# A two-block transformer step: activation stages at 512 columns, a third value stage in two half passes, and a new tail

## The reference

```
s1, s2 = q.k1, q.k2            # 8 heads, 128 keys each; top 16 of each, top 16 of the 256 sums
experts = e1 * 128 + e2        # 16,384 experts; gates = softmax(scores), 128 per token
a = einsum('td,tkd->tk', h, w_u[experts])
y = einsum('tk,tkd->td', gates * gelu(a), w_v[experts])
out = rmsnorm(x + y) * g_final
```

## Time and profile before

| | |
|---|---|
| Time, median of 3 runs | 3456.82 us (3452.38 to 3457.64) |
| Profiled execution: its own time, its span | 3448.67 us, 3446.9 us |
| PE busy, share of the span | 3105.9 us, 90% |
| DVE busy | 2007.6 us, 58% |
| ACT busy | 1343.6 us, 39% |
| POOL busy | 57.2 us, 2% |
| DMA, mean of the span | 155 GB/s |
| Mean granted TensorE clock | 0.954 of full |

### The profile page before, as it was taken

The page is one execution under the profiler, slowest core; times in us unless marked ns, Lnnn a source line. Parts: engine busy times, 40 slices in busy tenths (PEclk is TensorE's granted clock), DMA queues, the critical chain, the costliest instruction groups (busy, mean ns, idle before and its releaser), DMA issues. The chain is left out here.

```text
span 3446.9 us, 50034 instructions
## 1 busy us (share of the span) xinstructions
PE 3105.9 (90%) x20098; PEld 2737.8 (79%) x20098; DVE 2007.6 (58%) x2533; ACT 1343.6 (39%) x1461; POOL 57.2 (2%) x44
## 2 busy tenths in 40 slices
PE   6797895889987989898799889999999999999598
PEld 5675784678876778776699889988998889988486
DVE  3446456544566544444457967744775467744844
ACT  3434343444334443434434434434333433334044
POOL 0000000000000000000000000000000000000501
PEclk9898997999999999999899999999999999999699
DMA  5352453144443354344244444455444554455154
GB/s 215 127 185 86 146 198 120 54 167 168 161 150 110 122 183 177 135 171 147 100 163 167 158 147 158 169 183 193 163 166 166 191 181 164 164 181 191 55 193 136
DMA packets 80592, 535.34 MB, mean 155 GB/s; under 512 B 9960, under 2 KB 13664, under 8 KB 20064
## 3 DMA queue, kind: packets, MB, share of 16 engines
q1 hardware_dynamic: 72576, 520.98, 42.6%
q10 hardware_dynamic: 7904, 12.83, 1.1%
HBM read 530.57 MB, written 3.15 MB: 155 GB/s over the span
## 5 line engine op out<-in xcount | busy, mean ns | idle before, releaser
L1686 DVE TENSOR_TENSOR w_lo<-raw,w_hi 128x2048 fp32r<-128x2048 f32 (+2 forms) x500 | 1130.5, 2262 | 1210.8 <-ACT w_hi L1158 1208.5
L1158 ACT ACTIVATE w_hi<-raw 128x2048 fp32r<-128x2048 f32 (+2 forms) x500 | 945.2, 1891 | 1643.3 <-PE ps L642 660.0
L640 PE MATMUL ps<-w_hi,hT_hi 128*128 128x512 f32 (+3 forms) x1728 | 679.1, 393 | 84.7 <-DVEq L588 72.7
L641 PE MATMUL ps<-w_lo,hT_hi 128*128 128x512 f32 (+3 forms) x1728 | 669.4, 387 | 0.0
L642 PE MATMUL ps<-w_hi,hT_lo 128*128 128x512 f32 (+3 forms) x1728 | 668.6, 387 | 0.0
L1034 PE MATMUL ps<-hT_hi,w_hi 128*128 128x256 f32 x2048 | 590.3, 288 | 13.8 <-DVE w_lo L1686 10.6
L1035 PE MATMUL ps<-hT_lo,w_hi 128*128 128x256 f32 x2048 | 580.5, 283 | 0.0
L1036 PE MATMUL ps<-hT_hi,w_lo 128*128 128x256 f32 x2048 | 579.8, 283 | 0.0
L640 PEld LDWEIGHTS ps<-w_hi,hT_hi 128*128 128x128 f32 x1728 | 330.3, 191 | 157.1 <-DVEq L588 51.8
L1034 PEld LDWEIGHTS ps<-hT_hi,w_hi 128*128 128x128 f32 x2048 | 393.2, 192 | 19.7 <-issue 17.8
L1061 PE MATMUL ps<-w_hi,c_hi 128*128 128x512 f32 x1024 | 400.4, 391 | 6.9 <-DVE c_lo L2438 6.9
(11 more groups left out here) (246 smaller groups left out, 2574.8 us busy)
## 6 DMA issues: line engine op xcount, KB each, us to landing
raw<-in_w_u_t SPq DMA_DIRECT2D x128, 1024.0 KB, 4.7
raw<-in_w_v SPq DMA_DIRECT2D x128, 1024.0 KB, 5.2
raw<-in_w_in_2.0 SPq DMA_DIRECT2D x32, 1024.0 KB, 4.7
raw<-in_odd_w.0 SPq DMA_DIRECT2D x20, 1024.0 KB, 4.7
raw<-in_even_w.0 SPq DMA_DIRECT2D x20, 864.0 KB, 4.4
raw<-in_even_w.3608 SPq DMA_DIRECT2D x16, 1024.0 KB, 4.8
raw<-in_w_out.0 SPq DMA_DIRECT2D x16, 1024.0 KB, 4.8
raw<-in_w_out.1 SPq DMA_DIRECT2D x16, 1024.0 KB, 4.7
```

Of the source, the lines that this page charges most:

```text
L640: pe.matmul(o, hi, wh, start=(c == 0), stop=False)
L641: pe.matmul(o, hi, wl, start=False, stop=False)
L1158: act.activation(w_hi[:, s % 2, 0:size], raw[:, s, 0:size], ACT.Copy).then_inc(hi_done, 1)
L1686: dve.tensor_tensor(w_lo[:, s % 2, 0:size], raw[:, s, 0:size], w_hi[:, s % 2, 0:size].bitcast(F32), ALU.subtract).then_inc(lo_done, 1)
```

## The change

- **Activation stages 1 to 3** use one tile `hT` with `hi` and `lo` side by side: `w_hi` meets both in one matmul of 512 columns, `w_lo` meets `hT_hi` in one of 256, so an item has 32 matmuls in place of 48. The two halves of the bank are added by DVE (`add_halves`, a reduction over pairs, 512 values in and 256 out), and Gelu then works from SBUF in place. Stage 0 stays as it was.
- **The third value stage** (`HALVED` = 2) goes over its 32 rows twice, each pass with half of the columns of `w_v`; an item now holds two rows of 1024 columns, and there are again 32 items of 1 MB. A pass needs four banks, so two are free for the last part's gates, which are built between the two rows of each item. The stage of its own for the last gates is gone, and with it POOL's part in it. Only two banks are flushed, at the start of the second pass.
- **Tail:** POOL multiplies 1024 of the 2048 columns by `g_final`, DVE does the others together with the scaling in one operation; the square root's table is loaded ahead; the first statistics are made among the additions; SP issues two of the four stores. `g_final` is loaded at the start of the fourth value stage.

The core of the diff (PE, DVE and ACT of the value stage, and the activation stages; ACT's and SP's loops over passes are like PE's):

```diff
-    hT_hi = sb("hT_hi", [P, KC, S], F32R)
-    hT_lo = sb("hT_lo", [P, KC, S], F32R)
+    hT = sb("hT", [P, KC, 2, S], F32R)
+    hT_hi, hT_lo = hT[:, :, 0], hT[:, :, 1]
...
+            if (what, q) == ("V", HALVED):
...
+                            rows = src[bass.ds(8 * i + (q * QTR + 2 * s), 2)][:, :, 1024 * (1 - k):1024 * (2 - k)]
+                            sp.dma_start(raw[:, s].rearrange("p (a c) -> p a c", a=2), rows.rearrange("a p c -> p a c")
+                                         ).then_inc(landed[s], 16)
...
         def activations(i, s, q):
...
+            if q > 0:
+                pe.wait_ge(sums_done, 4 * i + ((q - 1) * QTR + s + 1))
+                for k in range(KC):
+                    pe.matmul(ps[:, s % 2, :], wh, hT[:, k].rearrange("p n t -> p (n t)"), start=(k == 0), stop=False,
+                              skip_group_check=True)
+                    mm = pe.matmul(ps[:, s % 2, 0:S], wl, hT_hi[:, k], start=False, stop=(k == KC - 1),
+                                   skip_group_check=True)
+                mm.then_inc(item_used, 1)
+                return
...
+        def half_outputs(i, s, k, first=False):
+            pe.wait_ge(lo_done, 4 * i + (v_first[HALVED] + 16 * k + s + 1))
+            for j in range(2):
+                if j == 1:
+                    if first and k == 1:
+                        pe.wait_ge(flushed, 4 * HALVED + 2)
+                    dense(i + 4 * k, s, PARTS - 1, 2 * k)
+                pe.wait_ge(c_lo_done, 8 * i + (c_first[HALVED] + 32 * k + 2 * s + j + 1))
+                for t in (1, 0):
...
+                    for m in range(2):
...
+                        pe.matmul(o, ch, wh, start=first and j == 0 and t == 0, stop=False, skip_group_check=True)
+                        pe.matmul(o, ch, wl, start=False, stop=False, skip_group_check=True)
+                        mm = pe.matmul(o, cl, wh, start=False, stop=False, skip_group_check=True)
+                mm.then_inc(item_used if j else c_used, 1)
...
+        def half_step(i, s, k, end=False):
+            half_high(i, s, k, 1)
+            split(i + (v_first[HALVED] // 4 + 4 * k + (s + 1) // 4), (s + 1) % 4, 2048)
+            if not (end and s == 3):
+                half_high(i + (s + 1) // 4, (s + 1) % 4, k, 0)
...
+        def add_halves(i, s, q):
+            dve.wait_ge(item_used, 4 * i + (u_first[q] + s + 1))
+            dve.tensor_reduce(CTS[q % 2][:, bass.ds(4 * i + s, 1)].rearrange("p a t -> p (a t)"),
+                              ps[:, s % 2, :].rearrange("p (n t) -> p t n", n=2), AX, ALU.add).then_inc(sums_done, 1)
...
+        def half_step(i, s, k, end=False):
+            half_low(i, s, k, 1)
+            if k == 1 and isinstance(i, int) and i + s == 0:
+                for b in (2, 3):
...
+                    dve.tensor_tensor(xs, xs, ps[:, b, :], ALU.add).then_inc(flushed, 1)
+            if not (closing and k == 1):
+                hots(i + 4 * k + (s + 1) // 4, (s + 1) % 4, g)
...
+            split(i + (v_first[HALVED] // 4 + 4 * k + (s + 1) // 4), (s + 1) % 4, 2048)
+            if not closing:
+                half_low(i + (s + 1) // 4, (s + 1) % 4, k, 0)
...
+            if not (closing and k == 1):
+                weigh(i + 4 * k, s, g, 2 * k)
...
+        for b in range(5):
+            bank_ends(b).then_inc(fin_add, 1)
+        variance(0)
+        bank_ends(5).then_inc(fin_add, 1)
+        inverse(0)
+        for b in range(6, 8):
+            bank_ends(b).then_inc(fin_add, 1)
...
+        scaled(0)
+        variance(1)
+        inverse(1)
+        scaled(1)
```

More of the change, by code:

```diff
@@ L179, in build_in @@
     bank_done = sem("bank_done")
+    c_used = sem("c_used")
     fin_add = sem("fin_add")
     fin_mul = sem("fin_mul")
+    fin_r = sem("fin_r")
     x_in = sem("x_in")
@@ L557, in _ @@
                                  ).then_inc(landed[s], 16)
+        for t in range(NT):
+            sp.wait_ge(dve_out, t + 1)
+            sp.dma_start(out[0, t * P:(t + 1) * P, 1024:2048], x[:, t, 1024:2048]).then_inc(out_done, 16)
     AT_MEM_ROOTS, AT_MEM_HEADS, AT_MEM_TURN, AT_MEM = 2, 3, 5, 7
@@ L1084, in _ @@
         for q in range(PARTS):
+            if q == HALVED:
+                for k in range(2):
+                    for s in range(RAW):
+                        half_outputs(0, s, k, s == 0)
+                    with pe.Fori(1, HLOOPS) as i:
+                        for s in range(RAW):
+                            half_outputs(i, s, k)
+                continue
             for s in range(RAW):
@@ L1611, in _, with half_high @@
         st.meet()
+        def half_high(i, s, k, j):
+            if j == 0:
+                act.wait_ge(c_used, 4 * i + (16 * k + s))
+            elif not isinstance(i, int) or 16 * k + 4 * i + s > 0:
+                act.wait_ge(item_used, 4 * i + (v_first[HALVED] + 16 * k + s))
+            act.activation(c_hi[:, j], CTS[HALVED % 2][:, bass.ds(8 * i + (2 * s + j), 1)].rearrange("p a t -> p (a t)"),
+                           ACT.Copy).then_inc(c_hi_done, 1)
+        def half_step(i, s, k, end=False):
[3 more added lines that the diff above has]
+                half_high(i + (s + 1) // 4, (s + 1) % 4, k, 0)
+            elif k == 0:
+                half_high(0, 0, 1, 0)
         for q in range(PARTS):
@@ L1656, in _ @@
     def _(pool):
[L1658 to L1665, removed]
-        pool.wait_ge(fin_in, 16)
[L1668 to L1672, removed]
+        pool.wait_ge(fin_in, 16)
+        for t in range(NT):
+            for b in range(4 * t, 4 * t + 2):
+                pool.wait_ge(fin_add, b + 1)
+                piece = slice((b % 4) * 512, (b % 4 + 1) * 512)
+                pool.tensor_tensor(XG[:, t, piece], x[:, t, piece], GFIN[:, piece], ALU.mult).then_inc(fin_mul, 1)
     @block.vector
@@ L2407, in step @@
                 if more:
-                    hots(i + (s + 1) // RAW, (s + 1) % RAW, g, q is None)
-                if q is not None and more:
+                    hots(i + (s + 1) // RAW, (s + 1) % RAW, g)
                     u_split(i, s, q)
+                elif g == HALVED:
+                    hots(0, 0, g + 1)
+                add_halves(i, s, q)
                 weigh(i, s, g)
[L2413 to L2417, removed]
+            hots(0, 0, g)
             with dve.Fori(0, LOOPS - 1) as i:
```

152 lines of the change are left out of this document (102 added, 50 removed).

## The result

The changed kernel takes 3400.4 us, median of 4 runs (3398.19 to 3401.74), beside 3454.95 of the kernel before: a ratio of 0.9845, 95% interval 0.9832 to 0.9857, so 54.5 us faster. The forecast was 3390, a gain of 67, with 3376 to 3412 as its range.

A forecast was written before the change was run, and what follows sets the result against it. PE was taken to bound the activation and value stages. Gains of 20.5, 43.0 and 3.5 us sum to 67, giving 3382 for the profiled execution and 3390 as the median, with 3376 to 3412 as the range.

The forecast's parts named there:

- rival A: Half passes: DVE's order sets the pace, costing 5 to 16 us, most likely 3400 us in all; chance 0.13.
- Part 2, the last gates in the half passes: Third value stage: gate stage's 65.5 us removed, gate groups add 23.4; net gain 43.0 us, V3's start included.
- the flush: Start of the third value stage's second pass: DVE flushes two banks and is late for the next item by 1.2 us.
- The chain: Half passes: the dependent steps of an item take 6.12 us where PE wants them at 6.17; it just fits.
- The loads in pieces of 4 KB: Third value stage: 1 MB loads land in between 5.2 and 6.0 us, hidden; zero cost.
- Part 1, the activation stages: Activation stages 1 to 3: an item's matmuls take 5.55 us for 5.76; gain 20.5 us over 96 items.
- Rival C: Activation stages: 512 columns cost nearly what two times 256 do, so a gain of 4 us, 3407 us; chance 0.04.
- Part 1, the chain: Activation stages: with table loads in each loop body, sums come at 12.9 us, needed at 13.3; no loss.
- rival B: Activation stages: a reduction of 1.2 us makes PE wait, costing 38 us over 24 bodies, 3428 us; chance 0.07.
- Part 3, the tail: From last matmul to last store: 6.2 us instead of 9.65, a gain of 3.5 us, between 1 and 6.
- V3's slow start: First 15 matmuls of the last value stage: 5.97 us would become 3.40, a gain of 2.6 us.
- Rival D: Half passes: the low clock comes in with the gates, 154 us more, 3544 us, slower than before; chance 0.03.

The follow-up runs named there:

- the kernel with all three edits: Changed kernel plus grouped widths, w_lo ahead of the one-hot operations, and a later third operation of the first gate group; the last run: 3390.76 us (0.9818).
- the grouped kernel: Changed kernel with each activation item's 16 matmuls of 512 columns first and its 16 of 256 columns behind them: 3393.75 us (0.9835).
- two and two: Changed kernel with activation matmuls in turns of two of 512 columns, then two of 256: 3397.8 us (0.9839).

## Why the prediction was nearly right

The sum was made for the profiled execution and gave 3382; that took 3398.19, 16 us more: 11.9 in part 1, 3.8 in part 2, 0.8 in the stages ahead. The median came within 10 of 3390 because it lay only 2 us above its profiled execution, where the forecast had added 8. That much is luck. And 3400 is where the prediction had put rival A, while what was found of A is 3.15 us.

**Part 2, the last gates in the half passes: right, and short by 3.8 us of 40.4.** The 65.5 us went, an item costs 5.44 plus 0.75 at best (6.19, predicted 6.17), the flush 1.25 (an item of 7.50 in the second run, against 6.25; predicted 1.2). The stage was to take 197.4 + 1.2 + 0.5 = 199.1 us and took 204.7. Of the 5.6 between, 3.15 is DVE's order, as the runs show (2.3 of it late `c_lo`, 0.9 the flush). The other 2.5 is a slow start at the low clock: in the kernel with all three edits, which has neither, V2 takes 199.11, the sum of the prediction. The kernel before had a slow start of 1.7 in the same place (3191.43 - 3015.65 = 175.8 for 174.1), so the gain fell short by 3.8 only. The chain was computed at 6.12 for a need of 6.17 and the margin was not there in every second item. Rival A was right in kind, and far smaller than its 5 to 16 us. The loads in pieces of 4 KB landed in 5.5 us against 5.2 of whole rows, inside the bounds, and nothing waited for them:

```profile
raw<-in_w_v SPq DMA_DIRECT2D x29, 1024.0 KB, 5.5
```

**Part 1, the activation stages: right in sign, the step that failed is the item's price.** "16 x (0.2267 + 0.12) = 5.55 us" took the step of each width from a stage in which that width stands alone. Alternating, the pair costs 0.354 us and an item 0.10 more; that is 9.6 us over 96 items, and the grouped kernel gave it back (0.347, 6.25). Another 1.2 us is U3's late end, below. The last 1.1 is in small things: even the grouped item gains 0.20 over the kernel before and not 0.213, and U1 and U2 end 0.15 us later each behind their last gate group (2.54 for 2.39). Rival C, which had part 1 bring 4 us and got a chance of 0.04, was nearer to the 8.6 than the forecast's 20.5, and what it says of the steps came true in kind: 0.236 for 512 columns in these stages, against 2 x 0.12. It did not name the cause, the alternation; 512 columns do cost 0.227 where they stand in a row. By the formula for an isolated matmul of the Trainium skill's page "TensorE: Matmul & The Clock Gate", section "Back-to-back issue gap", they would cost 0.216; the trace does not agree.

**Part 1, the chain.** It held, as forecast: PE waited nowhere for the reduction at 0.68 us. The 0.4 us that it was to have to spare were not measured by themselves. But it was walked as if every loop body reloaded ACT's tables; only U1's do, also in the kernel before. So rival B's 38 us at 1.2 us were too dear by more than three times: the doubled reduction cost 8.0 us in U1 and 0.7 and 1.2 elsewhere.

**Not in the prediction:** the last part's first gate group, put ahead of the last sums of U3, ends that stage 1.2 us late.

**Part 3, the tail: right.** From the last matmul to the last store 3392.50 - 3386.55 = 5.95 us, predicted 6.2. DVE's scaling took 1.28, predicted 1.15 with 1.3 as a bound:

```profile
3388.03 1.28 DVE L2606 SCALAR_TENSOR_TENSOR x<-x,small,work 128x1024 f32<-128x1024 f32 x1
...
3391.32 1.15 ACT L1736 ACTIVATE x<-work,small 128x1024 f32<-128x1024 f32 x1 [0.48 <-ACT x L1736]
3392.50 0.34 ACTq L1738 DMA_DIRECT2D out<-x  x1
```

**V3's slow start: right**, 2.48 of 2.6 us. **Rival D did not come:** V2's clock was 0.99 with the gates inside, and its 5 us at 0.50 lie at its start; behind the first gate group the 512-column step was 0.23 again.

## What to carry to other kernels

Take the price of a matmul from rows in which its neighbours are those it will have, and when two widths alternate, put those of one width together: here that doubled what the wider form brought in the activation stages (17.2 us for 8.6). When gate-like work moves into a stage, walk DVE's order for who is waited for, not only the sum: the same operations in another order gave 3 us. Give the clock's fall at a stage's start no place in a gain until several executions show it. Read a duration per stage from the trace when medians differ by less than their scatter.

## What the runs showed of the hardware

The same 32 matmuls take 5.66 us alternating between 512 and 256 columns (16 x 0.354), 5.57 two and two, and 5.55 in two runs. It was shown that the output half of the bank is not the cause (at most 0.5 us of a stage), nor the change of the stationary tile (see "Two and two"); what in the engine it is was not shown, and stays open.

The granted clock can fall to 0.50 for a few microseconds at the start of a value stage, after a pause that leaves it alone elsewhere. In the changed kernel V0 follows 1.77 us of idle PE and takes 174.71 us. In the last kernel it follows the same 1.77 us, and after a few matmuls the 512-column step goes from 0.23 to 2245.69 - 2245.26 = 0.43 us, the step of the 1.2 GHz level, for about seven matmuls:

```profile
2243.22 0.47 PE L1092 MATMUL ps<-w_hi,c_hi 128*128 128x512 f32 x1 [1.77 <-DVE c_lo L2555]
...
2245.26 0.63 PE L1093 MATMUL ps<-w_lo,c_hi 128*128 128x512 f32 x1
2245.69 0.63 PE L1094 MATMUL ps<-w_hi,c_lo 128*128 128x512 f32 x1
```

V0 and V1 take 176.31 there, 1.6 us more each, in the grouped kernel too. But with the sums in the other half of the bank only V1 is slow (176.30, V0 174.69), and with two and two only V0 (176.34, V1 174.71), all behind 1.77 us. The kernel before had its slow start at V2 alone, behind the same 1.63 us as V0 and V1. So neither the pause nor the stage's own code decides it. The two traces of the changed kernel agree in all three stages; of the others there is one each, and no more can be said. Up to 3 us at V0 and V1, and 2.5 at V2, hang on this and should not be put down to a change.
